# Moving the second weight sum behind the fourth role's remainder in a hybrid streaming encoder step (fp32, Strassen-Winograd feed-forward)

## What is computed

```python
def swiglu(x, w_gate, w_up, w_down):
    return (jax.nn.silu(x @ w_gate) * (x @ w_up)) @ w_down      # 1024 -> 2816 -> 1024
x = x + 0.5 * swiglu(rms_norm(x, g_norm[l, 0]), w_ffn_gate[l, 0], w_ffn_up[l, 0], w_ffn_down[l, 0])
```

## Time and profile before

| | |
|---|---|
| median of 3 runs | 2470.1 us (2469.92 to 2471.42) |
| the profiled execution | 2467.45 us |
| its span | 2465.4 us, granted clock 0.997 |
| PE busy | 2401.1 us (97%), 18377 matmuls |
| PEld busy | 2260.8 us (92%) |
| DVE busy | 1858.1 us (75%), 3710 instructions |
| ACT busy | 1332.9 us (54%), 2870 |
| POOL busy | 544.2 us (22%), 422 |

### The profile page before, as it was taken

The page is one execution under the profiler, slowest core; times in us unless marked ns, Lnnn a source line. Parts: engine busy times, 40 slices in busy tenths (PEclk is TensorE's granted clock), DMA queues, the critical chain, the costliest instruction groups (busy, mean ns, idle before and its releaser), DMA issues. The chain is left out here.

```text
span 2465.4 us, 48885 instructions
## 1 busy us (share of the span) xinstructions
PE 2401.1 (97%) x18377; PEld 2260.8 (92%) x18377; DVE 1858.1 (75%) x3710; ACT 1332.9 (54%) x2870; POOL 544.2 (22%) x422
## 2 busy tenths in 40 slices
PE   9899999999998999999999999999999999999998
PEld 8899999888678999999988999999996699999998
DVE  7888879322797888797925888887928878887865
ACT  6555556201885655555622655555618856555554
POOL 1222222354000121222144122222131002222210
PEclk9999999999999999999999999999999999999999
DMA  5657575333862465757424675766567544766642
GB/s 144 123 115 143 107 147 108 91 111 107 301 238 83 98 140 106 144 115 145 98 74 131 182 142 115 141 126 124 113 226 259 202 115 87 148 125 127 135 104 82
DMA packets 419397, 334.20 MB, mean 136 GB/s; under 512 B 20641, under 2 KB 379738, under 8 KB 418914
## 3 DMA queue, kind: packets, MB, share of 16 engines
q1 hardware_dynamic: 279376, 246.98, 32.3%
q0 software_dynamic: 133136, 65.82, 21.7%
q10 hardware_dynamic: 6658, 18.37, 2.0%
HBM read 314.98 MB, written 16.13 MB: 134 GB/s over the span
## 5 line engine op out<-in xcount | busy, mean ns | idle before, releaser
L976 PE MATMUL PS<-x_area,w_area 128*128 128x320 f32 x3096 | 483.8, 310 | 2.3 <-ACT PS L1778 2.3
L976 PEld LDWEIGHTS PS<-x_area,w_area 128*128 128x128 f32 x3096 | 462.4, 188 | 2.7 <-ACT PS L1778 2.6
L1692 ACT ACTIVATE w_area<-R 128x512 fp32r<-128x512 f32 (+2 forms) x583 | 325.3, 567 | 205.5 <-DVE R L2374 98.0
L2353 DVE TENSOR_TENSOR w_area<-R,w_area 128x512 fp32r<-128x512 f32 (+2 forms) x583 | 357.1, 615 | 96.8 <-ACT w_area L1692 95.4
L2353 DVE TENSOR_TENSOR r_area<-R,r_area 128x512 fp32r<-128x512 f32 (+2 forms) x437 | 269.6, 617 | 107.4 <-ACT r_area L1692 95.7
L1778 ACT ACTIVATE PS<-PS 128x320 f32<-128x320 f32 x438 | 177.1, 415 | 211.7 <-PE PS L976 180.5
L976 PE MATMUL PS<-r_area,w_area 128*128 128x320 f32 x1584 | 268.5, 312 | 10.7 <-ACT PS L1778 9.6
L1692 ACT ACTIVATE r_area<-R 128x512 fp32r<-128x512 f32 (+2 forms) x437 | 246.8, 568 | 53.1 <-DVE R L2374 35.7
L976 PEld LDWEIGHTS PS<-r_area,w_area 128*128 128x128 f32 x1584 | 240.3, 189 | 19.1 <-ACT PS L1778 15.4
L1202 PE MATMUL PS<-w_area,xn_hi 128*128 128x512 f32 x800 | 251.2, 395 | 1.7 <-DVE w_area L2344 1.7
L976 PE MATMUL PS<-r_area 128*128 128x320 f32 x1392 | 236.2, 310 | 3.0 <-DVE r_area L2608 1.8
(11 more groups left out here) (342 smaller groups left out, 4132.0 us busy)
## 6 DMA issues: line engine op xcount, KB each, us to landing
R<-in_w_ffn_up_dram SPq DMA_DIRECT2D x45, 512.0 KB, 5.2
R<-in_w_ffn_gate_dram SPq DMA_DIRECT2D x43, 512.0 KB, 4.7
R<-in_w_ffn_up_dram SPq DMA_DIRECT2D x86, 256.0 KB, 3.7
R<-in_w_ffn_up_dram POOLq DMA_DIRECT2D x86, 256.0 KB, 5.0
R<-in_w_ffn_gate_dram SPq DMA_DIRECT2D x82, 256.0 KB, 4.6
R<-in_w_ffn_gate_dram POOLq DMA_DIRECT2D x81, 256.0 KB, 5.4
R<-in_w_ffn_down_dram SPq DMA_DIRECT2D x52, 384.0 KB, 4.0
R<-in_w_ffn_down_dram SPq DMA_DIRECT2D x88, 192.0 KB, 3.3
```

The costliest lines, as they stand in the source:

```text
L976: last = pe.matmul(PS[:, bank, 0:HT], a[:, k, :], b, start=(start and opens), stop=(k == n - 1 and a is lo), skip_group_check=True)
L1692: act.activation(role_parts(f, g, s, role)[0], role_source(f, g, s, role), ACT.Copy).then_inc(sem("early_cast") if key in EARLY_COUNT else ...
L2353: dve.tensor_tensor(lo, role_source(f, g, s, role), hi.bitcast(F32), ALU.subtract).then_inc(sem("early_split") if key in EARLY_COUNT else ...
```

## The change

The sum of the next set's S2 (with its wait for S4's remainder) stands directly behind S4's remainder on DVE: in `ffn_sets` ahead of the hidden sums 5, 7 and 6 and of S3's remainder, in `opening_down` ahead of the remainder of hidden part 4. `first_late` is false everywhere, so in all down sets the next set's W11 is rounded (ACT) and its remainder made (DVE) ahead of S4 and S3; the plan's counts follow.

```diff
 def first_late(at):
-    return is_down(*at) and not opens_down(*at) and GROUPS[at[0]] == 2
+    return False
...
                 role_low(f, *cur, "S3")
                 role_low(f, *cur, "S4")
-                hidden_lows(f, *prev, "4")
                 dve.wait_ge(w_split, SPLIT[(f, *cur, "S4")])
                 role_sum(f, *then, "S2")
+                hidden_lows(f, *prev, "4")
                 role_low(f, *then, "S1")
...
                     role_low(f, *cur, "S4")
+                    if then is not None:
+                        dve.wait_ge(w_split, SPLIT[(f, *cur, "S4")])
+                        role_sum(f, *then, "S2")
                     if turned:
                         hidden_sums(f, *prev, ("5", "7", "6"))
                     if n and not third_first(f, cur):
...
                     if then is not None and first_late(cur):
                         role_low(f, *then, "W11")
                     if then is not None:
-                        dve.wait_ge(w_split, SPLIT[(f, *cur, "S4")])
-                        role_sum(f, *then, "S2")
                         role_low(f, *then, "S1")
```

## The result

The changed kernel takes 2477.7 us in the median of 8 runs (2474.4 to 2484.0), the kernel before beside it 2465.93 (8 runs). The recorded ratio is 1.0051, interval 1.004 to 1.0062 (1.0048 by the two medians): **+11.8 us, slower**. The forecast was +9.3 us, 2479.4 with a range of 2472.0 to 2485.0. The profiled execution of after took 2476.77 us; forecast for it 2476.8.

The account below looks back on a forecast made before the run. TensorE was taken to bound the kernel, so only its idle gaps count. The terms +14.1 + 0.6 - 4.4 - 1.0 gave +9.3 us on 2470.1, so 2479.4 us, range 2472.0 to 2485.0.

Parts of the forecast that it names:

- Part 1: Turned sets (gate sets following an up set): early sum delays hidden sums and copy 2, +14.1 us over 24 sets.
- The three sets without spare: Three turned sets where TensorE already waits for copy 2: the full 0.73 us shift shows as a gap.
- Part 2: Other sets, sum ahead of S3's remainder: mostly hidden under waits, +0.6 us from eleven second down sets of three-pair groups.
- The openings: The 15 sets that open a group: sum passes hidden part 4's remainder; taken as 0, bounds -2 and +2 us.
- The gate sets behind a down set: Copy 2 ends 1.35 us ahead of its product there, so the early sum costs 0.
- Part 3: Down sets of two-pair groups, W11 first: shorter gaps, -1.1 us a layer, -4.4 in all, bounds 0 and -12.0.
- "third" set: Third of three two-pair down sets priced: copy 2 loses W11's 0.52 us, gap falls 1.37 to about 0.5.
- the dearer case: Two-pair down sets: W11's rounding waits for its near quarter, blocks S4's; 12 sets lose some 0.5 us each, total 2485.
- Part 4: Third layer's turned set with a late load: load issued 0.6 us earlier, -1.0 us, between 0 and -2.45.
- Rival 2: Two sides cancel: earlier loads give down sets and late load their full gain, +0.3 us, 2470.4; chance 0.14.
- Rival 3: Turned sets' chain has more room, so the early sum costs nothing there: faster, 2456.2 to 2465.3 us; chance 0.04.
- rival 4: The change does nothing, as S2's sum may wait for its own inputs at its old place; chance 0.02.

Follow-up runs that it names:

- x1: The kernel before, with the early sum in the 25 turned sets (gate sets following an up set) alone: 2480.7 us, ratio 1.0055.
- x4: The changed kernel with W11 late as before, so only the sum moved, in every set: 2477.5 us, ratio 1.0039 to before.
- x2: The changed kernel with the sum back behind hidden sums and S3's remainder in turned sets: 2464.3 us, ratio 0.9994 to before.
- x6: The changed kernel, with ScalarE in turned sets rounding S3 and making copy 2 ahead of the hidden parts' casts: 2465.2 us, ratio 1.0000 to before.
- x5: The changed kernel with hidden sum 5 ahead of S2's sum in turned sets: 2477.8 us, ratio 1.0056 to before.
- x3: The kernel before, with only W11 first in the down sets of two-pair groups: 2465.7 us, ratio 0.9994.
- x9: The kernel before, with the sum early except in non-opening down sets, and copy 2 straight behind S3's rounding in turned and down sets: 2456.5 us, ratio 0.9971.
- x10: x9 with copy 2 behind W11's rounding in the second to fourth down sets of two-pair groups: 2455.1 us, ratio 0.9966 to before.

## Why the prediction was right, and where it was not

**Part 1, the turned sets (+14.1 forecast): right.** In the 24 sets the gaps grew from 0.48 to 14.82, +14.3 us; x1, which has the early sum in the turned sets alone, lost 13.6 us in time. The price of the new pair was the term that mattered, taken from the one pair in the trace at 0.73; measured 0.72. The gap is 0.54 to 0.55 in 21 sets, as forecast. The three sets without spare were given 0.73 and have 0.67, 0.90 and 1.83, the last of them by something that was not followed up (the same set has 0.86 in x1 and 0.68 in x4). The Trainium skill's rule ("VectorE: DVE Perf Modes", "The DRAIN you can't avoid": a semaphore between Vector operations costs nothing extra, found there on a chain of eight copies) would have given 11.0 us for this part. Here the measurement decides against it: 0.72 with the wait, 0.60 without.

**Part 2 (+0.6 and 0): right.** The second down sets of three-pair groups went from 5.88 to 6.44, +0.56. S3's remainder does meet the product, as the text said (in after, the set that answers to the earlier trace rows):

```profile
990.19 0.55 DVE L2353 TENSOR_TENSOR w_area<-R,w_area 128x384 fp32r<-128x384 f32 x1
...
990.86 0.88 PEld L976 LDWEIGHTS PS<-r_area,w_area 128*128 128x128 f32 x6 [0.48 <-issue]
990.89 1.11 PE L976 MATMUL PS<-r_area,w_area 128*128 128x320 f32 x6 [0.25 <-DVE w_area L2353]
```

The openings, priced at 0, gave 1.6 back ahead of S2 in the set behind them (2.13 to 0.53) and took 0.4 ahead of S1 (0.64 to 1.01): -1.2, inside the bounds. The gate sets behind a down set, priced at 0 too, have one gap of 0.94 ahead of S3 (second layer), behind a W11 rounding that waited 3.02 for its load. The third and fourth down sets of three-pair groups, for which the prediction had no term, have three such gaps, 1.50 in all. Before and in x1, where the sum moves in turned sets alone, there is none of either kind; x2 to x6 have 0.3 to 2.1 us of them, not always in the same sets.

**Part 3, the two-pair down sets (-4.4): the step that failed.** The gaps ahead of S3 did not fall by 4.4 us: they are 2.0 longer in after, and 0.0 to 1.2 longer in x2, x5 and x6, which have the same down sets. The prediction's "third" set, the fourth down set, was to go from 1.37 to about 0.5, since copy 2 "loses the 0.52 of W11". It does; copy 2 is done 0.98 us early, and the gap is still 1.36. For the product then waits for S3's remainder, which I had seen as the limit in the first two of the three sets only. And "nothing in the rows shows that quarter late" was the wrong test: before, W11's rounding stood behind S3's, which itself waited for a load, so the rows could not show whether its own weights were there. They come 1.38 us late in this layer and 2.51 in the fourth. It is the dearer case that stood beside the forecast, but not in all 12 sets: the fourth down sets lost 2.2 us in all, 1.5 of it in the fourth layer's; the second ones lost 0.8, and the third gained 1.0.

**Part 4, the late load (-1.0): right in the gap.** The idle time fell by 1.02 (2.70 to 1.68), and in x1 and x4, with the early sum in this set too, by 1.3. The twelve loads behind it fell by 1.26 as well, since the clock stayed at its upper level: together 2.3, close to the bound of -2.45. But x3 has the long gap and no slow loads, so this 1.26 may have come without the change.

**Sum.** The forecast had 14.1 + 0.6 - 4.4 - 1.0 = +9.3. Measured in gaps, the same terms are 14.3 + 0.6 + 2.0 - 2.3, with -1.2 for the openings: +13.4. The 2.4 us in sets that were put at nothing, or not priced at all, make it +15.8, and the sum over all loads, taken by itself, is +15.5. The layers of the profiled execution grew by 14.5 us and not by 9.3; that it took 2476.77 us where 2476.8 was forecast is luck, for the code outside the layers happened to run 5 us shorter. Of the medians the same holds more mildly: the difference is +11.8, and the 2479.4 stood on a kernel before of 2470.1 (3 runs), which is 2465.9 over 8. The forecast was right in sign by part 1, whose mechanism and price x1, x2 and x6 bear out. That the difference comes within 2.5 us of the forecast is in part luck, since the other misses partly cancelled.

Rival 2 (the two sides cancel) needed the parts beside the turned sets at their full gain, near -14 us; x2 has just these parts and comes out at -0.06%, -1.5 us, with an interval to -3.7. Rival 3 (more room in the chain) falls with x1, rival 4 with x1 and the change itself.

## What to carry to other kernels

Before moving work forward on an in-order engine, follow the first thing behind it through the other engines to the one that bounds the kernel, and read the slack there, not where the wait stands: 0.72 us on VectorE, which is idle a quarter of the time, cost 0.55 us on TensorE 21 times. What took the loss away here was to take the urgent instruction (a copy of 0.42 us, with the rounding ahead of it) out from behind the late ones; what gained (x9 and x10) was to do that and to keep the early sum only where it had shortened gaps. And an instruction that stands behind a wait in the old trace does not show whether its own inputs are there: before it is put first, look up when its load lands.

## What was not expected of the hardware

- Two VectorE operations of 128x512 start 0.60 us apart when the second waits for nothing, and 0.72 apart when it waits for the first (928.55 behind 927.83; 926.90 behind 926.18 in x6). Put one other operation between them, as in x5, and the sum starts 0.40 behind that one, as close as hidden sums follow each other.
- A short wait can cost twice, but need not: behind the idle 2.70 us of the earlier trace rows TensorE was granted 0.63 of its clock in the mean of 4 us, so in part its lower level of 1.2 GHz, and twelve loads took 3.03 us; behind the idle 2.65 us of the same set in x3 it kept 1.00 and they took 1.77.
- Two changes on the same path do not add up by themselves. In the fourth down sets of the two-pair groups W11 first cost 1.7 us alone and the early sum alone gained 0.8, and both together cost 0.9 to 2.2.
